# A decoder block's MLP on Trainium2: one of the Strassen-like weight sums moves from accumulating transfers to the vector engine

## What is computed

```python
h2 = rmsnorm(x, g_mlp[l])
u = jax.nn.relu(jnp.einsum('bsd,df->bsf', h2, w_ff1[l]))      # 1024 -> 4096
x = x + jnp.einsum('bsf,fd->bsd', u * u, w_ff2[l])            # 4096 -> 1024
```

## Time and profile before

| | us |
|---|---|
| median of three runs (lowest, highest) | 376.05 (375.89, 376.48) |
| profiled execution, its own time | 375.65 |
| span of the profiled execution | 373.8 |
| PE busy | 361.7 (97%) |
| DVE busy | 279.5 (75%) |
| ACT busy | 228.4 (61%) |
| POOL busy | 41.3 (11%) |

### The profile page before, as it was taken

One profiled execution on the slowest core, in us unless ns is written; L12 is line 12 of the kernel. 1 busy time (PEld: TensorE's weight loads), 2 busy tenths in 40 slices (PEclk: granted clock), 3 DMA queues, 4 the chain that ended last, 5 costly groups with the idle time before them and its releaser, 6 DMA issues.

```text
span 373.8 us, 5645 instructions
## 1 busy us (share of the span) xinstructions
PE 361.7 (97%) x2176; PEld 314.2 (84%) x2176; DVE 279.5 (75%) x378; ACT 228.4 (61%) x368; POOL 41.3 (11%) x61
## 2 busy tenths in 40 slices
PE   5899999999999999999999999999999999999993
PEld 5898889876787777888889899999999999999983
DVE  0976973956747654669377869989998888998484
ACT  4995425966665656145184557767777676666424
POOL 4222000000000100000120111021111111220002
PEclk9999999999999999999999999999999999999998
DMA  7998657775241355308536799889999998963002
GB/s 240 367 390 255 261 176 232 217 241 177 95 155 29 105 218 207 122 0 250 202 111 203 176 377 256 244 252 315 291 276 273 281 270 266 285 174 115 0 2 112
DMA packets 43910, 76.79 MB, mean 205 GB/s; under 512 B 2880, under 2 KB 22080, under 8 KB 43632
## 3 DMA queue, kind: packets, MB, share of 16 engines
q1 hardware_dynamic: 38528, 66.59, 52.5%
q0 software_dynamic: 4176, 9.64, 12.9%
q10 hardware_dynamic: 1184, 0.27, 0.3%
HBM read 75.44 MB, written 1.05 MB: 205 GB/s over the span
## 4 chain that ended last, share of the span: by engine, by line
PE 92%; ACT 2%; DVE 2%; DMA 1%; issue 1%; POOL 0%; POOLq 0%; SPq 0%; ACTq 0%; DVEq 0%
PE ps L1298 28%; PE ps L1300 28%; PE ps L1299 28%; PE ps L1305 4%; PE ps L1419 2%; PE ps L1445 2%; DMA xs<-in_x_dram 1%; ACT prob L636 1%; DVE negmax L962 1%; PE ps L1410 1%; ACT xT_hi L499 0%; POOL qkT_b L486 0%; ACT prob L499 0%; DVE wlo L851 0%; DVE xT_lo L915 0%
## 5 line engine op out<-in xcount | busy, mean ns | idle before, releaser
L499 ACT ACTIVATE whi<-raw 128x1024 fp32r<-128x1024 f32 (+3 forms) x124 | 119.5, 1008 | 21.6 <-PE ps L1300 16.8
L851 DVE TENSOR_TENSOR wlo<-raw,whi 128x1024 fp32r<-128x1024 f32 (+3 forms) x68 | 73.7, 1118 | 19.4 <-ACT whi L499 19.3
L1298 PE MATMUL ps<-whi,xT_hi 128*128 128x512 f32 (+3 forms) x208 | 79.0, 380 | 1.9 <-DVE wlo L851 1.6
L1300 PE MATMUL ps<-whi,xT_lo 128*128 128x512 f32 (+3 forms) x208 | 75.6, 363 | 0.0
L1299 PE MATMUL ps<-wlo,xT_hi 128*128 128x512 f32 (+3 forms) x208 | 75.3, 362 | 0.0
L1300 PE MATMUL ps<-xT_hi,wlo 128*128 128x256 f32 x224 | 63.4, 283 | 0.0
L1299 PE MATMUL ps<-xT_lo,whi 128*128 128x256 f32 x224 | 63.4, 283 | 0.0
L1298 PE MATMUL ps<-xT_hi,whi 128*128 128x256 f32 x224 | 63.3, 283 | 0.0
L1298 PE MATMUL ps<-whi,lat_hi 128*128 128x512 f32 (+2 forms) x134 | 51.8, 387 | 0.0
L1299 PE MATMUL ps<-wlo,lat_hi 128*128 128x512 f32 (+2 forms) x134 | 51.3, 382 | 0.0
L1300 PE MATMUL ps<-whi,lat_lo 128*128 128x512 f32 (+2 forms) x134 | 51.1, 382 | 0.0
(11 more groups left out here) (141 smaller groups left out, 481.9 us busy)
## 6 DMA issues: line engine op xcount, KB each, us to landing
raw<-in_w_ff_dram SPq DMA_DIRECT2D x32, 1024.0 KB, 7.1
raw<-in_w_in_dram SPq DMA_DIRECT2D x14, 1024.0 KB, 6.0
raw<-in_w_out_dram SPq DMA_DIRECT2D x4, 1024.0 KB, 5.0
t_raw<-in_w_ff_dram SPq DMA_DIRECT2D x12, 256.0 KB, 7.7
raw<-in_w_ff_dram POOLq DMA_DIRECT2D x12, 256.0 KB, 5.2
t_raw<-in_w_ff_dram POOLq DMA_DIRECT2D x12, 256.0 KB, 7.0
gates<-in_b_gate_dram POOLq DMA_DIRECT2D x2, 1024.0 KB, 6.3
raw<-in_w_o_a_dram SPq DMA_DIRECT2D x2, 1024.0 KB, 4.9
```

The source lines that it names most:

```text
L499: return nc.scalar.activation(dst, src, ACT.Copy, scale=scale)
L851: nc.vector.tensor_tensor(wlo[:, s, h * w:(h + 1) * w], raw[:, s, h * w:(h + 1) * w], whi[:, s, h * w:(h + 1) * w].bitcast(F32), ALU.subtr ...
L1298: nc.tensor.matmul(dst, a_hi, b_hi, start=start, stop=False)
L1300: return nc.tensor.matmul(dst, a_lo, b_hi, start=False, stop=stop)
```

## The change

T3 = B12 + B22 is made by DVE from the landed slot (`block_sum3`), and the second load of B12 and the accumulating transfer of B22 are gone. The sum reads B12 before T1's transfer overwrites it, so L461 now waits for the sum's semaphore `t3_ready` instead of raw's landing, and DVE waits for the landing. `block_sum3(c + p, 1 - p)` stands in `low_w2(c, p)` between `low_blocks` (L1110, L1113) and `low_sums` (L1118, L1121), so it is the sum of the next half. The first two, for (1, 0) and (1, 1), are in the entry: one behind the second square, one behind `low_blocks(1, 0)`.

```diff
--- before.py
+++ after.py
@@ -249,9 +249,8 @@
         w2_lo = sem("w2_lo")
         last_hi = sem("last_hi")
         last_lo = sem("last_lo")
-        t3_landed = [sem(f"t3_landed{p}") for p in range(2)]
         t1_summed = [sem(f"t1_summed{p}") for p in range(2)]
-        t3_summed = [sem(f"t3_summed{p}") for p in range(2)]
+        t3_ready = sem("t3_ready")
         t_part = sem("t_part")
         t24_ready = sem("t24_ready")
         s_part = sem("s_part")
@@ -363,8 +362,6 @@
                     sp.wait_ge(w2_lo, 4 * (2 * (c - 2) + p) + 4)
                 sp.dma_start(ff_slot(2 + p).rearrange("p (f n) -> p f n", f=2),
                              w2_rows(c, p)).then_inc(raw_landed[(U_FF + 2 + p) % SLOTS], 16)
-                if 1 <= c < FAST:
-                    sp.dma_start(t3_raw[:, p, :], w2_rows(c, p)[:, 0, HALF:D]).then_inc(t3_landed[p], 16)
 
             for t in range(TT):
                 sp.dma_start(xs[:, t, :], x_v[:, t, :]).then_inc(x_landed[t], 16)
@@ -457,12 +454,9 @@
 
                 s = (U_FF + 2 + p) % SLOTS
                 rows_of = w_ff2[0, c * HALF + p * 256:c * HALF + (p + 1) * 256, :].rearrange("(f p) n -> p f n", p=P)
-                pool.wait_ge(raw_landed[s], 16 * ((U_FF + 2 + p) // SLOTS + 1 + c))
+                pool.wait_ge(t3_ready, 2 * c + p - 1)
                 pool.dma_start(raw[:, s, HALF:2 * HALF], rows_of[:, 0, 0:HALF], accum_op=ALU.add)\
                     .then_inc(t1_summed[p], 16)
-                pool.wait_ge(t3_landed[p], 16 * c)
-                pool.dma_start(t3_raw[:, p, :], rows_of[:, 1, HALF:D], accum_op=ALU.add)\
-                    .then_inc(t3_summed[p], 16)
 
             for t in range(TT):
                 first = ssq[:, SSQ_MLP + 2 * t:SSQ_MLP + 2 * t + 1]
@@ -740,7 +734,7 @@
                 copy(t24_hi[p], t24_raw[:, :, :].rearrange("p a b -> p (a b)")).then_inc(w2_hi, 1)
 
             def high_t3(c, p):
-                act.wait_ge(t3_summed[p], c * 16)
+                act.wait_ge(t3_ready, c * 2 + p - 1)
                 copy(t3_hi[p], t3_raw[:, p, :]).then_inc(w2_hi, 1)
 
             def high_last(p):
@@ -1113,6 +1107,13 @@
                 nc.vector.tensor_tensor(wlo[:, s, 0:w], raw[:, s, 0:w], whi[:, s, 0:w].bitcast(F32),
                                         ALU.subtract).then_inc(w2_lo, 1)
 
+            def block_sum3(c, p):
+
+                s = (U_FF + 2 + p) % SLOTS
+                dve.wait_ge(raw_landed[s], c * 16 + 16 * ((U_FF + 2 + p) // SLOTS + 1))
+                nc.vector.tensor_tensor(t3_raw[:, p, :], raw[:, s, T1 * HALF:(T1 + 1) * HALF],
+                                        raw[:, s, B22 * HALF:(B22 + 1) * HALF], ALU.add).then_inc(t3_ready, 1)
+
             def low_sums(p, n):
                 dve.wait_ge(w2_hi, n + 1)
                 nc.vector.tensor_tensor(t24_lo[p], t24_raw[:, :, :].rearrange("p a b -> p (a b)"),
@@ -1121,8 +1122,10 @@
                 nc.vector.tensor_tensor(t3_lo[p], t3_raw[:, p, :], t3_hi[p].bitcast(F32),
                                         ALU.subtract).then_inc(w2_lo, 1)
 
-            def low_w2(c, p):
+            def low_w2(c, p, last=False):
                 low_blocks(c, p, c * 8 + 4 * p - 8)
+                if not last:
+                    block_sum3(c + p, 1 - p)
                 low_sums(p, c * 8 + 4 * p - 6)
 
             def low_last(p):
@@ -1211,7 +1214,7 @@
                     lefts_low(c, 0)
                     low_w1(c + 1, 0, (1,))
                 block_sums(c, 1)
-                low_w2(c, 1)
+                low_w2(c, 1, last)
                 left_sums(c, 1)
                 low_w1(c + 1, 1, (0,))
                 lefts_low(c, 1)
@@ -1235,12 +1238,14 @@
             u_rows_low(0)
             low(U_FF + 3, 1)
             square(0, 1)
+            block_sum3(1, 0)
             low_w1(1, 0)
             u_rows_low(1)
             low_w1(1, 1)
             block_sums(1, 0, first=True)
             low_sums(0, 0)
             low_blocks(1, 0, 2)
+            block_sum3(1, 1)
             add_rows0(0)
             mlp_chunk(1, first=True)
             with dve.Fori(2, FAST - 1) as c:
```

## The result

The changed kernel took **376.75 us** in the median of 20 runs (376.55 to 378.19). The kernel before, run beside it, took 376.10 us (20 runs, 375.89 to 376.87). The ratio is 1.002, with a 95% interval of [1.0013, 1.0026], so the changed kernel is slower by 0.2%, clear of the noise, though no more than what the prediction named as the least that can be told from no change. The forecast was 376.0 us and no change; 376.75 lies inside its range of 375.3 to 376.9.

A forecast was written before the change was run, and what follows sets the result against it. PE's own instructions were taken as the bound from 200 us to the final rows. With 0 removed and 0 added the time stayed 375.65 us; the forecast against the median was 376.0 us, range 375.3 to 376.9.

The forecast's parts named there:

- Removed: 12 issues on SP: Edited stage: dropping 12 issues each on SP and POOL and 6.3 MB of traffic gains 0 on the path.
- the sum: Whole run: 0 removed and 0 added leave 375.65 us, span 373.8 plus 1.85 around it.
- the 7% for slower: Whole run: chance of a slower result, 4% DVE-bound through the moved transfer, 7% with half-way cases.
- The sum hides: MLP stage, DVE: 12 added sums, 7.3 us of work, fit under PE's 10.61 us period; cost 0.
- the third rival's picture: DVE loop: DVE already behind, 10.24 us a period, slack near 4 to 5 us, same time; no separate chance.
- Slack of PE's products over 3 us everywhere: Edited stage: sign expected in the profile, DVE's results over 3 us ahead of PE's products.
- the worst early case: Load issued behind (1, 1) takes 9.4 us to land; 3.7 us of slack before PE are left.
- The entry: First two sums: slip the low parts 0.3 us, leaving 0.9 us before PE, the smallest slack.
- The wait for the landing: DVE's new wait for raw: landing taken as 6.5 us, bounds 4.8 and 9.4; cost 0 at both.
- The rival's half-way case: A load landing above 8 us, or the entry's 0.9 us used up, makes it slower; included in 7%.
- The moved transfer: T1's accumulation (L461) waits for the sum, starting 0.7 to 1.7 us later; median landing 5.2 us, cost 0.
- the DVE-bound rival: Moved transfer makes DVE the bound if T1's landing averages over 6.7 us; about 385 us, 4%.

The follow-up runs named there:

- x_gone: Kernel before without T3's two transfers and with no sum in their place (B12 left out of the third sum): 376.59 us, ratio 1.0019.
- the pads: Changed kernel plus already-met waits on POOL (12, 24 or 48), SP (12 or 24) or both: 376.00 to 376.39 us.
- p_both: Changed kernel plus 24 already-met waits on POOL and 12 on SP: 376.09 us, ratio 1.0002.
- k_sums: Kernel before plus 12 dead vector sums on DVE into a spare tile, without the landing wait, all transfers kept: 376.03 us, ratio 1.0001.
- n_after: Changed kernel run again, unchanged: 376.63 us, ratio 1.0023 to the kernel before.
- p_sp12: Changed kernel plus 12 already-met waits on SP behind its last w2 load: 376.39 us, ratio 1.0007.
- n_before: Kernel before run again, unchanged: 376.40 us, ratio 1.0007.
- x_kept: Changed kernel with T3's load and accumulation still issued into an unread spare tile, plus an ordering wait on SP: 379.56 us, ratio 1.01.

## Why the prediction held for most of the stage and failed in its sign

**The direction came out wrong, in two of its steps.** "Removed: 12 issues on SP ... and 12 on POOL ... Worth on the path: 0" counted what these instructions do while the kernel runs, and that was indeed 0. It did not count that the instructions are also the program's length; their removal cost 0.65 us. And the sum, "375.65 us, the time of the profiled execution (span 373.8 plus 1.85 around it)", carried the 1.85 us around the span over as a constant. It measured 2.53 in the changed kernel and accounts for the whole loss (2.53 - 1.82 = 0.71, against 0.65 between the medians). x_gone has the loss with nothing but the removal; the pads take it away with nothing but instructions. That the removal is the cause is shown in this sense. That fetches behind the last instruction are how it comes about is argued: it rests on the late packets going with it, 0 of them wherever the time around the span was 1.81 to 1.84 us and 2 wherever it was 2.3 to 2.5, and p_both, with one late packet and no loss in all, does not fit. None of the rivals named the place, so the 7% for slower was not for this mechanism, and it should not be read as foresight. That the median lay inside the range is no merit of the mechanism either: the range's slightly longer side was for waits, and no wait made this loss.

The Trainium skill (Runtime: NRT & Kernel Launch, Instruction fetch mechanics) says that a sequencer fetches the next page of its program while it executes the present one, in blocks of 16 KiB, and that crossing a boundary is "mostly hidden". This case's trace agrees that the fetches inside the span cost nothing to be seen; the packets of q14 are about 8 KB here (0.07 MB over 8). Two fetches behind the span go with 0.5 to 0.7 us more around it, and there the measurement decides.

**Point by point, the rest.** The costs came out as forecast in the median; two readings behind them did not.

- *The sum hides.* DVE was busy for 286.6 us (forecast 288) and k_sums showed the 12 sums at no cost. The sums stand back to back in the steady loop, in DVE's timeline, where the gap before the last low part has gone as well:

```profile
284.19 0.69 DVE L1114 TENSOR_TENSOR t_raw<-raw 128x512 f32<-128x512 f32 x1
284.80 1.22 DVE L1119 TENSOR_TENSOR t_lo<-t_raw,t_hi 128x1024 fp32r<-128x1024 f32 x1
285.93 0.69 DVE L1122 TENSOR_TENSOR t_lo<-t_raw,t_hi 128x512 fp32r<-128x512 f32 x1
...
296.13 0.68 DVE L1122 TENSOR_TENSOR t_lo<-t_raw,t_hi 128x512 fp32r<-128x512 f32 x1
```

  The period from one L1122 to the next is 10.20 us, for a predicted 10.24. DVE runs nearly without idle time, which is the third rival's picture, called there the likeliest form.

- *The slack was misread.* The prediction took L1121, the last low part of w2, for what PE's products wait for last, with 5.6 us of slack at (1, 1) and 7.9 in the loop. The products of (c, 1) also wait for the left factor of their own half, which `lefts_low` makes after `low_w2`. The kernel before made it here:

```profile
236.54 1.09 DVE L1150 TENSOR_TENSOR lat_lo<-rows,lat_hi 128x896 fp32r<-128x896 f32 x1
```

  It ended at 237.63, and PE began at 240.03: 2.4 us. In the loop it was 293.06 - 288.30 = 4.8 us (L1150 at 287.21). The changed kernel's two:

```profile
237.57 1.09 DVE L1153 TENSOR_TENSOR lat_lo<-rows,lat_hi 128x896 fp32r<-128x896 f32 x1
...
288.66 1.08 DVE L1153 TENSOR_TENSOR lat_lo<-rows,lat_hi 128x896 fp32r<-128x896 f32 x1
```

  The slack was 240.45 - 238.66 = 1.8 us at (1, 1) and 293.48 - 289.74 = 3.7 us five periods later: 0.39 us gained in each, for 0.37 predicted. "Slack of PE's products over 3 us everywhere" was thus false, and of the 3.7 us that the worst early case had left, some 0.5 remain, as the left factor ended 3.16 us behind L1122 (238.66 - 235.50).

- *The entry.* From these rows of DVE's timeline:

```profile
211.22 0.68 DVE L1231 TENSOR_TENSOR lat_lo<-ps,lat_hi 128x512 fp32r<-128x512 f32 x1
...
220.71 0.68 DVE L1114 TENSOR_TENSOR t_raw<-raw 128x512 f32<-128x512 f32 x1
...
225.00 1.09 DVE L1153 TENSOR_TENSOR lat_lo<-rows,lat_hi 128x896 fp32r<-128x896 f32 x1 [1.08 <-ACT lat_hi L493]
```

  L1231 (before, L1228) ended at 211.90 and PE began at 212.87: 0.97 us, for a predicted 0.9. The left factor ended at 226.09, 3.75 us ahead of PE. The second sum did not wait for its landing in this run; it waited 1.63 us in n_after, 3.61 in p_sp12 and 3.47 in p_both.

- *The wait for the landing.* The load landed in 6.8 us in the median, up to 8.6 (by line, 200 to 360 us), where 6.5 was taken, and in this trace DVE did not wait. "Cost: 0 at both ends" is right for the median, where the span stayed 374.2, and wrong for single executions. Its upper bound, 9.4 us, was that of a single trace. The load of (1, 1) took 11.8 us in the same kernel before in another run and up to 12.6 in the changed one's padded forms, with the relief; DVE then waited 3.5 or 3.6 us against a slack of 1.8, and PE was 1.4 or 1.6 us behind the changed kernel. The rival's half-way case, "a load that lands above 8 us", names this wait; it did not make the loss of the median.

- *The moved transfer.* T1's accumulation started behind the sum and landed in 4.0 us in the median (3.8 to 6.0), faster than the 5.2 that the sum used; the point at which the DVE-bound rival decides, 6.7 us, was never near. The estimate of 2.6 us by the Trainium skill's fit was too short in both traces.

- *Relief gives PE nothing.* Right: the traffic's share fell by 0.3 in the same stretch and PE's 10.60 us stayed.

## What to carry to other kernels

Keep the time around the span apart from the span when runs are compared; a loss that no engine shows may lie there, and a view of the transfers behind the last instruction tells whether the chip was still fetching program. Removed instructions are not free by definition: when a change takes instructions off a queue, look at the instruction packets before and after, and test with waits that are already met before blaming the work that the change added. A wait on a transfer is hidden or not by the slowest landing, and one trace does not show it: look at the landings of several traces and at the longest spans of all runs, and try the wait with the old traffic too. When slack is counted, go through every wait of the consumer in the code and take the one that is met last.

## What the runs showed of the chip that was not expected

- **A late fetch.** Without late instruction packets the time around the span was 1.81 to 1.84 us in every kernel; with two it was 2.34 to 2.53 (1.91 with pads on SP), with one 2.01 to 2.06 (1.56 with pads on both). The two in brackets have 0.26 us more inside the span.
- **The start varies.** Two runs of one program began their first transposes at 6.77 and 7.21 us and had spans of 373.8 and 374.7, so one trace against one trace cannot show 0.4 us.
- **One load varies most.** The longest landing of a w2 load (1024 KB) was 7.9 us in one trace and 12.6 in another, with medians of 5.0 to 8.1. In the five traces where it was above 10 us (n_before, n_after, x_kept, p_sp12, p_both) it was the load of (1, 1).
- **DVE is stretched beside POOL.** A DVE operation on two tensors of SBUF took much longer while POOL's gain row (128x1024, 3.1 to 3.5 us) ran: L1121 of the same shape took 0.93 us in the kernel before, L1122 1.38 in the changed one, 2.46 in k_sums and L1132 2.63 in x_kept, where 0.69 is the rule; the 1.22 us form took 2.31 in n_before and 2.77 in x_gone. From the timeline of DVE and of POOL of the changed kernel:

```profile
326.77 3.13 POOL L474 TENSOR_SCALAR qkT_b<-qkT_b 128x1024 f32<-128x1024 f32 x1
...
327.32 1.38 DVE L1122 TENSOR_TENSOR t_lo<-t_raw,t_hi 128x512 fp32r<-128x512 f32 x1 [0.28 <-ACT t_hi L493]
```

  The Trainium skill (SBUF — State Buffer, Who interferes with whom) states that a DVE instruction with two SBUF inputs contends with a GpSimd instruction that reads SBUF. The trace agrees: up to 1.9 us were lost by one instruction. It was harmless in every kernel with slack on DVE and cost 1.3 us of PE's time in x_kept, which had none.
